# A weight ring of eight 2 MB places turned into four places of 4 MB

## The chip, the cores and the metric

The kernel runs on one core of a Trainium2 chip. The metric is the device time of one execution in microseconds (us). A core has five engines that run side by side: TensorE (PE in the rows; its weight loads are listed apart as PEld), VectorE (DVE), ScalarE (ACT), GpSimd (POOL) and SyncE (SP). Here SP mostly issues transfers. Sixteen DMA engines move the data; each transfer is spread over all of them, and a transfer adds 16 to its semaphore when it has landed.

## The reference

One decoder layer is computed for 256 prompt tokens and 8 sample tokens, 264 in all, with a model width of 1024, in float32. An attention and a recurrent branch are added to the input. Then each token goes through 4 of 32 experts and the results are added:

```
x += mix(x)
x += sum over the token's top 4 of 32 experts: gate * expert(rmsnorm(x))
expert(v) = act(v @ w_gate_up) @ w_down      # w_gate_up 1024 x 2048, w_down 1024 x 1024
```

The activation is a clamped SwiGLU of the gate and the up columns. One expert's weights are 8 MB (gate-up) and 4 MB (down), so 32 experts have 384 MB, each byte of which is read once. With 64 token slots to an expert, no expert overflows in these inputs.

## The kernel before

The first 172 us compute the two branches, the router and the choice of tokens. After that TensorE works through 16 pairs of experts. A pair gathers 64 tokens for each of two experts into one tile of 128 and transposes it (`x_transposes`). For each of the two experts it then does `gate_up` (line 1554: 32 matmuls of 64 tokens by 512 columns, contraction in 8 blocks of 128, and 4 bias matmuls), `act_transposes` (line 1575: 4 transposes of 128 by 128 that turn the activated tile around) and `down` (line 1582: 16 matmuls). Beside the matmuls VectorE and ScalarE compute the activation and copy results out of PSUM. Between the two halves of a pair TensorE adds the results of the pair before to the tokens (`place_half`, `place_quarters`, lines 1596 to 1605) and gathers the tokens of the next pair (line 1493). In the trace one float32 matmul is two MATMUL instructions, and one transpose is one.

The weights come through a ring of eight places of 2 MB: six in a buffer of their own, one in the tail of `regA`, one in the head of `regX`. An expert is six pieces: four of gate-up, which hold two consecutive rows per partition, and two of down, with four rows per partition. SP issues piece n+8 when TensorE has counted piece n as used (`m_used`); TensorE counts a gate-up piece after 8 matmuls and a down piece after 8. TensorE waits for a piece by the semaphore of its place (`landed`, line 1545).

Before the experts start the ring is filled as far as memory is free. Pieces 0 to 3 are issued at the start. Pieces 4 and 5 lie where the attention branch had its scratch (`scr`) and are issued when that branch is done. Pieces 6 and 7 lie in `regX` and `regA` and are issued when the router is done. From then on the loop at line 343 takes over:

```
sp.wait_ge(m_used, u * (4 * PIECES) + (n + 1))
load_piece(n % SLOTS, u * 4 + x, j)
```

Of the kernel before, what the change touches and what calls it, by code (L numbers as in the profile page):

```python
# [25 lines left out]
P = 128  # L26
D = 1024
KT = D // P
NP_ = 256
NS = 8  # L30
T = NP_ + NS
# [4 lines left out]
NC = 4  # L36
# [3 lines left out]
FF = 1024  # L40
D_IN = 1792
CAP = 64
N_OVER = 16
ITEMS = E + N_OVER
PIECES = 6
GU = 4
SLOTS = 8
PIECE = 4 * FF
POS0 = 4096
EPS = 1e-6  # L50
SCALE = HD ** -0.5
# [23 lines left out]
def hybrid_layer(nc, a, o):  # L75

    ctx = ExitStack()
    with ctx:
        def sb(name, shape, dt=F32):
            return ctx.enter_context(nc.sbuf_tensor(name, shape, dt))  # L80
# [1 line left out]
        def sem(name):  # L82
            return ctx.enter_context(nc.semaphore(name))

        ring = sb("ring", [P, 6, PIECE])
        regA = sb("regA", [P, KT * D_IN + 5 * T + NC * (3 + NP_)])
        con = sb("con", [P, NCONST])
        x_row = sb("x_row", [P, NT, D])
        xq = sb("xq", [P, D // 4])
        regX = sb("regX", [P, KT * T + 2 * NC * T])  # L90
        hT_t = regX[:, 0:KT * T]
        regC = regX[:, KT * T:]
        regD = regA[:, KT * D_IN:]
# [24 lines left out]
        ps = ctx.enter_context(nc.psum_tensor("ps", [P, 8, 512], F32))  # L118
# [4 lines left out]
        ident = cc("ident")  # L123
# [20 lines left out]
        up_sb = regA[:, 3072:3584]  # L144
        sig_sb = regA[:, 3584:4096]
        act_sb = regA[:, 4096:4608]
        actT = regA[:, 4608:5120].rearrange("p (j t) -> p j t", j=4)

        y_sb = [regA[:, 2048:2560], regA[:, 5120:5632]]

# [5 lines left out]
        xg = x_row[:, 2, :]  # L156
# [10 lines left out]
        idxg = chosen(694, 3)  # L167
        tail = KT * D_IN + 5 * T + NC * (3 + NP_)

        slot = [ring[:, s, :] for s in range(6)] + [regA[:, tail - PIECE:tail], regX[:, 0:PIECE]]  # L170

        def at(x, j):
            return divmod(PIECES * x + j, SLOTS)

        scr = ring[:, 4:6, :].rearrange("p s n -> p (s n)")
        diag_x = [scr[:, P * i:P * i + P] for i in range(NT)]
        v0 = scr[0:KT, 384:512]
        st10 = scr[0:10, 1400:1400 + T]
# [39 lines left out]
        s_slot = [sem(f"slot_landed{j}") for j in range(SLOTS)]  # L218
# [45 lines left out]
        def _(sp):  # L264
# [28 lines left out]

            def load_piece(s, e, j):
                if j < GU:
                    src = w_gu[bass.ds(e * D + j * 2 * P, 2 * P), :].rearrange("(p t) n -> p t n", t=2)
                    sp.dma_start(slot[s].rearrange("p (t n) -> p t n", t=2), src).then_inc(s_slot[s], 16)
                else:
                    src = w_dn[bass.ds(e * FF + (j - GU) * 4 * P, 4 * P), :].rearrange("(p t) n -> p t n", t=4)
                    sp.dma_start(slot[s].rearrange("p (t n) -> p t n", t=4), src).then_inc(s_slot[s], 16)  # L300

            def load_first(i):
                load_piece(i, i // PIECES, i % PIECES)

            for i in range(4):
                load_first(i)

            sp.wait_ge(S["proj"], 14)
# [13 lines left out]

            sp.wait_ge(S["pv"], 2)
            sp.wait_ge(S["ms_o"], 1)
            load_first(4)
            sp.wait_ge(S["s_pv"], 1)
            sp.wait_ge(s_cout, 32)
            load_first(5)

            sp.wait_ge(S["out_r"], 5)  # L330
            for odd in range(2):
# [2 lines left out]
            sp.dma_start(tokens, a["tokens"][:, :]).then_inc(s_tok, 16)  # L334
            sp.dma_start(bias_dn, a["b_down"][0]).then_inc(s_tok, 16)
            sp.wait_ge(S["logit"], NT)
            load_first(7)
            sp.wait_ge(S["xn"], 1)
            sp.wait_ge(S["xw"], 6)
            sp.wait_ge(S["st_tr"], 3)  # L340
            load_first(6)

            with sp.Fori(0, E // 4 - 1) as u:
                for n in range(4 * PIECES):
                    x, j = divmod(SLOTS + n, PIECES)
# [133 lines left out]
        def _(act):  # L479
# [204 lines left out]

            def copy_act(q):
                act.wait_ge(m_atr, q + 1)
                act.activation(actT[:, :, :], ps[:, 3, :].rearrange("p (j t) -> p j t", j=4),
                               ACT.Copy).then_inc(m_aT, 1)

            def bias_gu(odd, e):  # L690
# [32 lines left out]
            with act.If(n_over > 0):  # L723
                with act.Fori(0, n_over) as m:
                    for odd in range(2):
                        e = act.value_load(ovi[0:1, bass.ds(m * 2 + 1 + odd, 1)], min_val=0, max_val=E - 1)
# [463 lines left out]
        def _(pe):  # L1190
            def transpose(out, in_, k):
                return pe.transpose(out, in_, ident[0:k, 0:k])  # L1192
# [32 lines left out]
            for n in range(len(order) + 1):  # L1225
# [9 lines left out]
                kt = order[n - 1]  # L1235
# [4 lines left out]
                for m in range(6):  # L1240
                    mm = product(m, 2 + m, kt)
# [44 lines left out]
            for n, w in ((0, 128), (1, 256)):  # L1286
                for c in range(4):
                    for g in range(2):
                        h = 4 * g + c
                        out = ps[:, 2 + h // 2, 256 * (h % 2):256 * (h % 2) + 256] if n else ps[:, 6 + g, P * c:P * c + P]  # L1290
                        mm = pe.matmul(out, qk[64 * g:64 * g + 64, c, P * n:P * n + P],
                                       qk[64 * g:64 * g + 64, 4, 0:w], start=True, stop=True)
# [43 lines left out]
            for j, (n, kb, g) in enumerate(groups):  # L1336
# [43 lines left out]
            for b in range(NS):  # L1380
                r = slice(8 * b, 8 * b + 8)
# [145 lines left out]
            def x_transposes(g, half):  # L1527

                pe.wait_ge(m_xr, 2 * g + (half + 1))
                pe.sem_inc(m_passed, 1)  # L1530
                for j in range(4):
                    c = 512 * half + 2 * P * (j // 2) + j % 2
                    mm = transpose(ps[:, 7 - half, P * j:P * j + P], xg[:, c:c + 2 * P - 1:2], P)
                mm.then_inc(m_xtr, 1)

            def slot_sums():
# [8 lines left out]
            def landed(r, x, j, over):  # L1545

                again, s = at(x, j)
                if over:
                    pe.wait_ge(s_slot[s], r * (32 if s < 2 * PIECES - SLOTS else 16) + (E // 4 * 48 + 16 * again + 16))
                else:  # L1550
                    pe.wait_ge(s_slot[s], r * 48 + (16 * again + 16))
                return slot[s]

            def gate_up(p, r, x, over):

                odd = x % 2
                for kt in range(KT):
                    if kt % 2 == 0:
                        w = landed(r, x, kt // 2, over)
                    for n in range(2):  # L1560
                        for h in range(2):
                            c = 2048 * (kt % 2) + 1024 * h + 512 * n
                            mm = pe.matmul(ps[64 * h:64 * h + 64, 1 + n, :], xT[:, kt, 64 * odd:64 * odd + 64],  # L1563
                                           w[:, c:c + 512], start=(kt == 0), stop=False)
                    if kt % 2:
                        mm.then_inc(m_used, 1)
                pe.wait_ge(s_bgu[odd], p * 32 + 32)
                pe.sem_inc(m_passed, 1)
                for n in range(2):
                    for h in range(2):  # L1570
                        mm = pe.matmul(ps[64 * h:64 * h + 64, 1 + n, :], selb[32 * n:32 * n + 2, h, :],  # L1571
                                       b_gu[odd][32 * n:32 * n + 2, :], start=False, stop=True)
                mm.then_inc(m_gu, 1)

            def act_transposes(q):

                pe.wait_ge(m_act, q + 1)
                for j in range(4):
                    mm = transpose(ps[:, 3, P * j:P * j + P], act_sb[:, j:j + 4 * P - 3:4], P)
                mm.then_inc(m_atr, 1)  # L1580

            def down(p, r, x, over, ahead=False):

                pe.wait_ge(m_aT, p * 2 + (x % 2 + 1))
                for h in range(2):
                    w = landed(r, x, GU + h, over)
                    for j in range(4):
                        for n in range(2):
                            mm = pe.matmul(ps[64 * n:64 * n + 64, 4, :], actT[:, j, 64 * h:64 * h + 64],  # L1589
                                           w[:, 1024 * j + 512 * n:1024 * j + 512 * n + 512],  # L1590
                                           start=(h == 0 and j == 0), stop=(h == 1 and j == 3))
                    mm.then_inc(m_used, 1)
                    if ahead and h == 0:
                        x_transposes(p + 1, 1)

            def place_quarters(lhs, rhs):

# [156 lines left out]
```

## Time and profile before

| what | us |
|---|---|
| median of three runs | 1121.16 (1119.91 to 1129.12) |
| the profiled execution, its own time | 1119.43 |
| span of its trace | 1117.5 |
| TensorE busy in the span | 1062.6 |
| VectorE, ScalarE, GpSimd busy | 323.7, 152.3, 53.6 |
| DMA read from memory | 420.06 MB, 378 GB/s over the span |

Times inside the trace count from the start of the span. What lies around it is 1.9 us. Matmuls are pipelined, so that a TensorE that is shown as busy may still have room. Where TensorE waits for a piece, the row of the matmul tells so in brackets with the idle time before it.

### The profile page before, as it was taken

Reading aid. Unit: us, or ns where it says so; the run is one execution under the profiler, and the core shown is the slowest. Engines: PE = TensorE matmul, PEld = TensorE weight load, DVE = VectorE, ACT = ScalarE, POOL = GpSimd, SP = SyncE. Lnnn points to the kernel's source line nnn. Section 1 sums busy time; section 2 is a strip of 40 time slices with the busy share of each in tenths; the row PEclk is TensorE's granted clock in tenths of the full one; section 3 lists DMA queues with packets and bytes.
Section 4 is the critical chain, followed back from the end, with each engine's and each line's share of the span. In section 5 each row is a group of like instructions: output and inputs, shape, how many; then the busy total and the mean of one; then the engine's idle time right before and its main releaser. Section 6 shows DMA issues by size and latency. Waiting matters only on the chain.

```text
span 1117.5 us, 12869 instructions
## 1 busy us (share of the span) xinstructions
PE 1062.6 (95%) x4987; PEld 429.5 (38%) x4987; DVE 323.7 (29%) x653; ACT 152.3 (14%) x284; POOL 53.6 (5%) x85
## 2 busy tenths in 40 slices
PE   5999988999999999999999999999999999999996
PEld 4676453343333343433332333333333333233322
DVE  1482569113131313131313131313131312213132
ACT  1145331010101010101010101010101101010100
POOL 4063020000000000000000000000000000000000
PEclk9999888899999999999999999999999999999998
DMA  9906327699999999999999999999999999999991
GB/s 334 382 17 180 151 103 308 287 425 429 427 428 427 427 429 427 429 429 427 429 428 427 428 429 428 427 428 428 428 428 428 428 428 430 427 428 428 426 427 72
DMA packets 33020, 421.75 MB, mean 377 GB/s; under 512 B 4466, under 2 KB 4962, under 8 KB 8398
## 3 DMA queue, kind: packets, MB, share of 16 engines
q1 hardware_dynamic: 31486, 418.34, 89.2%
q0 software_dynamic: 1264, 2.75, 0.8%
q8 instruction: 21, 0.34, 0.1%
q10 hardware_dynamic: 240, 0.25, 0.1%
q14 instruction: 9, 0.07, 0.0%
HBM read 420.06 MB, written 2.33 MB: 378 GB/s over the span
## 4 chain that ended last, share of the span: by engine, by line
PE 67%; DMA 28%; DVE 3%; issue 1%; ACT 0%; SPq 0%; DVEq 0%; ACTq 0%
DMA ring<-in_w_gate_up_dram 26%; PE ps L1563 24%; PE ps L1589 15%; PE ps L1493 8%; PE ps L1216 3%; PE ps L1192 3%; PE ps L1605 3%; PE ps L1390 3%; PE ps L1571 2%; PE ps L1219 2%; DMA regA<-in_w_out_dram 1%; PE ps L1540 1%; PE ps L1202 1%; DMA x_row<-in_x_prompt_dram 1%; PE ps L1408 0%
## 5 line engine op out<-in xcount | busy, mean ns | idle before, releaser
L1563 PE MATMUL ps<-ring,regA 128*64 128x512 f32 x1536 | 341.5, 596 | 22.4 <-DMA ring<-in_w_gate_up_dram 22.3
L1563 PEld LDWEIGHTS ps<-ring,regA 128*64 128x64 f32 x1536 | 108.6, 137 | 249.9 <-issue 203.8
L1589 PE MATMUL ps<-ring,regA 128*64 128x512 f32 x768 | 173.4, 601 | 0.1
L1142 DVE TENSOR_SCALAR regA<-ps 128x512 f32<-128x512 f32 x32 | 22.1, 691 | 422.2 <-PE ps L1571 422.2
L683 ACT ACTIVATE regA<-regA 128x512 f32<-128x512 f32 x32 | 20.2, 630 | 675.2 <-DVE regA L1142 675.2
L1156 DVE COPY regA<-ps 64x512 f32<-64x512 f32 x64 | 44.1, 688 | 205.2 <-PE ps L1589 204.2
L1589 PEld LDWEIGHTS ps<-ring,regA 128*64 128x64 f32 x768 | 53.1, 138 | 106.6 <-issue 98.7
L1493 PE MATMUL ps<-regA 128*128 128x512 f32 x192 | 88.5, 610 | 0.0
L1605 PE MATMUL ps<-regA 128*128 128x512 f32 (+1 forms) x136 | 69.2, 634 | 0.0
L1563 PE MATMUL ps<-regX,regA 128*64 128x512 f32 x256 | 58.0, 595 | 0.5 <-DMA regX<-in_w_gate_up_dram 0.2
L1563 PE MATMUL ps<-regA 128*64 128x512 f32 x256 | 57.6, 592 | 0.0
L1493 PEld LDWEIGHTS ps<-regA 128*128 128x128 f32 x192 | 35.8, 193 | 51.0 <-issue 51.0
L1136 DVE TENSOR_TENSOR x_row<-x_row,ps 128x512 f32<-128x512 f32 x68 | 42.4, 682 | 4.5 <-PE ps L1605 3.9
L1216 PE MATMUL ps<-regX,regA 128*128 128x264 f32 x160 | 39.2, 395 | 0.0
L1571 PE MATMUL ps<-regA,con 2*64 2x512 f32 x256 | 34.8, 613 | 0.0
L1605 PEld LDWEIGHTS ps<-regA 128*128 128x128 f32 (+1 forms) x136 | 24.3, 199 | 26.0 <-issue 26.0
L1390 PE MATMUL ps<-regA,regX 128*128 128x512 f32 x64 | 31.8, 649 | 1.4 <-DMA regA<-in_w_out_dram 1.4
L1216 PEld LDWEIGHTS ps<-regX,regA 128*128 128x128 f32 x160 | 29.8, 192 | 8.4 <-issue 3.9
L1563 PEld LDWEIGHTS ps<-regX,regA 128*64 128x64 f32 x256 | 17.6, 137 | 39.2 <-issue 31.4
L1563 PEld LDWEIGHTS ps<-regA 128*64 128x64 f32 x256 | 18.4, 137 | 36.6 <-issue 36.6
L1589 PE MATMUL ps<-regA 128*64 128x512 f32 x128 | 30.8, 625 | 0.7 <-issue 0.7
L1192 PEld LDWEIGHTS ps<-con,regA 128*128 128x128 f32 (+3 forms) x141 | 21.5, 195 | 20.6 <-DVE regA L1150 9.4
(280 smaller groups left out, 717.3 us busy)
## 6 DMA issues: line engine op xcount, KB each, us to landing
ring<-in_w_gate_up_dram SPq DMA_DIRECT2D x96, 2048.0 KB, 29.8
ring<-in_w_down_dram SPq DMA_DIRECT2D x48, 2048.0 KB, 34.3
regX<-in_w_gate_up_dram SPq DMA_DIRECT2D x16, 2048.0 KB, 29.9
regA<-in_w_gate_up_dram SPq DMA_DIRECT2D x16, 2048.0 KB, 29.2
regA<-in_w_down_dram SPq DMA_DIRECT2D x8, 2048.0 KB, 34.0
regX<-in_w_down_dram SPq DMA_DIRECT2D x8, 2048.0 KB, 35.4
regA<-in_w_in_dram SPq DMA_DIRECT2D x8, 896.0 KB, 12.2
regA<-in_w_out_dram SPq DMA_DIRECT2D x2, 1024.0 KB, 10.5
```

What stands on the lines that cost most here:

```text
L1136: dve.tensor_tensor(half, half, ps[:, PLACE[i][h], :], ALU.add).then_inc(m_add, 1)
L1142: dve.tensor_scalar(g_sb, gu[:, 0::2], LIMIT, None, ALU.min).then_inc(m_g, 1)
L1156: dve.tensor_copy(y_sb[n][64 * odd:64 * odd + 64, :], ps[64 * n:64 * n + 64, 4, :]).then_inc(m_ysb, 1)
L1192: return pe.transpose(out, in_, ident[0:k, 0:k])
L1216: return pe.matmul(ps[:, bank, 0:T], w_in[:, kt, P * n:P * n + P], hT[:, kt, :], start=(kt == 0), stop=(kt == KT - 1))
L1219: mm = pe.matmul(ps[64 * g:64 * g + 64, bank, 0:T], w_in[:, kt, 256 * g + 64 * n:256 * g + 64 * n + 64], hT[:, kt, :], start=(kt == 0), st ...
L1390: mm = pe.matmul(ps[:, bank, :], src[:, c, P * i:P * i + P], w_out[:, NC * half + c, 512 * n:512 * n + 512], start=(c == 0), stop=(c == NC ...
L1493: return pe.matmul(ps[:, 5 * half, :], oneh[:, i, :], xn_row[:, i, 512 * half:512 * half + 512], start=(i == 0), stop=(i == 1))
L1563: mm = pe.matmul(ps[64 * h:64 * h + 64, 1 + n, :], xT[:, kt, 64 * odd:64 * odd + 64], w[:, c:c + 512], start=(kt == 0), stop=False)
L1571: mm = pe.matmul(ps[64 * h:64 * h + 64, 1 + n, :], selb[32 * n:32 * n + 2, h, :], b_gu[odd][32 * n:32 * n + 2, :], start=False, stop=True)
L1589: mm = pe.matmul(ps[64 * n:64 * n + 64, 4, :], actT[:, j, 64 * h:64 * h + 64], w[:, 1024 * j + 512 * n:1024 * j + 512 * n + 512], start=(h ...
L1605: return pe.matmul(ps[:, PLACE[i][h], :], lhs[:, P * i:P * i + P], rhs[h], start=True, stop=True)
```

## The change

The ring has four places of 4 MB. Three are in a buffer of their own; the fourth joins the tail of `regA` to the head of `regX`, which are now one tensor. An expert is three pieces: two of gate-up with four rows per partition, and the whole down block with eight rows per partition. The same bytes are in the ring and the same bytes are moved, in 96 transfers instead of 192. A piece is counted as used after 16 matmuls instead of 8.

With eight rows per partition the down block needs the activated tile in another order. The 4 transposes become 16 ordinary matmuls with the identity on 64 by 64 quarters of the array: for each of eight column offsets one for each half of the partitions. A semaphore increment is added in front of them. The token transposes step by four columns instead of two.

```
-PIECES = 6
-GU = 4
-SLOTS = 8
-PIECE = 4 * FF
+PIECES = 3
+GU = 2
+SLOTS = 4
+PIECE = 8 * FF
...
-        slot = [ring[:, s, :] for s in range(6)] + [regA[:, tail - PIECE:tail], regX[:, 0:PIECE]]
+        slot = [ring[:, s, :] for s in range(3)] + [regAX[:, tail - PIECE // 2:tail + PIECE // 2]]
...
             def load_piece(s, e, j):
                 if j < GU:
-                    src = w_gu[bass.ds(e * D + j * 2 * P, 2 * P), :].rearrange("(p t) n -> p t n", t=2)
+                    src = w_gu[bass.ds(e * D + j * 4 * P, 4 * P), :].rearrange("(p t) n -> p t n", t=4)
...
-                    src = w_dn[bass.ds(e * FF + (j - GU) * 4 * P, 4 * P), :].rearrange("(p t) n -> p t n", t=4)
+                    src = w_dn[bass.ds(e * FF, FF), :].rearrange("(p t) n -> p t n", t=8)
...
-            for i in range(4):
+            for i in range(2):
                 load_first(i)
...
             sp.wait_ge(S["pv"], 2)
             sp.wait_ge(S["ms_o"], 1)
-            load_first(4)
             sp.wait_ge(S["s_pv"], 1)
             sp.wait_ge(s_cout, 32)
-            load_first(5)
+            load_first(2)
...
             sp.wait_ge(S["logit"], NT)
-            load_first(7)
             sp.wait_ge(S["xn"], 1)
             sp.wait_ge(S["xw"], 6)
             sp.wait_ge(S["st_tr"], 3)
-            load_first(6)
+            load_first(3)
...
                 for j in range(4):
-                    c = 512 * half + 2 * P * (j // 2) + j % 2
-                    mm = transpose(ps[:, 7 - half, P * j:P * j + P], xg[:, c:c + 2 * P - 1:2], P)
+                    c = 512 * half + j
+                    mm = transpose(ps[:, 7 - half, P * j:P * j + P], xg[:, c:c + 4 * P - 3:4], P)
...
                 for kt in range(KT):
-                    if kt % 2 == 0:
-                        w = landed(r, x, kt // 2, over)
+                    if kt % 4 == 0:
+                        w = landed(r, x, kt // 4, over)
...
-                    if kt % 2:
+                    if kt % 4 == 3:
                         mm.then_inc(m_used, 1)
...
             def act_transposes(q):
 
                 pe.wait_ge(m_act, q + 1)
-                for j in range(4):
-                    mm = transpose(ps[:, 3, P * j:P * j + P], act_sb[:, j:j + 4 * P - 3:4], P)
+                pe.sem_inc(m_passed, 1)
+                for t in range(8):
+                    for h in range(2):
+                        r = slice(64 * h, 64 * h + 64)
+                        mm = pe.matmul(ps[r, 3, 64 * t:64 * t + 64], act_sb[r, t:t + 8 * 64 - 7:8], ident[r, r], start=True, stop=True)
                 mm.then_inc(m_atr, 1)
 
             def down(p, r, x, over, ahead=False):
 
                 pe.wait_ge(m_aT, p * 2 + (x % 2 + 1))
-                for h in range(2):
-                    w = landed(r, x, GU + h, over)
-                    for j in range(4):
-                        for n in range(2):
...
-                    mm.then_inc(m_used, 1)
-                    if ahead and h == 0:
+                w = landed(r, x, GU, over)
+                for t in range(8):
+                    for n in range(2):
+                        mm = pe.matmul(ps[64 * n:64 * n + 64, 4, :], actT[:, t, :], w[:, 1024 * t + 512 * n:1024 * t + 512 * n + 512],
+                                       start=(t == 0), stop=(t == 7))
+                    if ahead and t == 3:
                         x_transposes(p + 1, 1)
+                mm.then_inc(m_used, 1)
```

## Rows read from the trace of the kernel before

**Rows 1.** The page: DMA's busy share in tenths, in 40 slices of the span.
```profile
DMA  9906327699999999999999999999999999999991
```

**Rows 2.** Busy time by stretch; last three columns: granted clock, DMA share, GB/s.
```profile
core 0: us, PE busy (x) PEld busy (x) DVE busy (x) ACT busy (x) POOL busy (x), PEclk, DMA share, GB/s
...
200.00:210.00 10.00, 10.00 (x38) 2.97 (x38) 1.78 (x3) 0.00 (x0) 0.00 (x0) 0.80 0.24 70
210.00:220.00 10.00, 10.00 (x48) 3.23 (x46) 1.63 (x4) 0.00 (x0) 0.00 (x0) 1.00 1.00 429
220.00:230.00 10.00, 10.00 (x42) 4.05 (x39) 2.67 (x4) 1.64 (x3) 0.00 (x0) 1.00 1.01 432
250.00:1050.00 800.00, 779.41 (x3564) 282.57 (x3562) 190.02 (x347) 81.46 (x125) 0.00 (x0) 1.00 1.01 428
...
1090.00:1100.00 10.00, 6.33 (x32) 2.08 (x29) 2.67 (x4) 1.23 (x2) 0.00 (x0) 0.91 0.17 72
```

**Rows 3.** The chain of waits by time: start, length, what (gate-up is L1563).
```profile
239.00 13.73 PE ps L1563 x64
...
519.03 13.73 PE ps L1563 x64
...
575.00 6.89 PE ps L1563 x32
582.05 32.56 DMA ring<-in_w_gate_up_dram
...
634.12 6.89 PE ps L1563 x32
...
1049.81 6.89 PE ps L1563 x32
```

**Rows 4.** SP's timeline, 100 to 216 us: issues of weight pieces, merged.
```profile
112.77 0.82 SPq L300 DMA_DIRECT2D ring<-in_w_down_dram  x2
...
160.36 0.37 SPq L297 DMA_DIRECT2D regA<-in_w_gate_up_dram  x1
177.80 3.73 SPq L297 DMA_DIRECT2D ring<-in_w_gate_up_dram  x2
184.62 3.80 SPq L300 DMA_DIRECT2D ring<-in_w_down_dram  x2
206.69 3.30 SPq L297 DMA_DIRECT2D ring<-in_w_gate_up_dram  x2
```

**Rows 5.** TensorE's timeline, 170 to 215 us: transposes and down of expert 0.
```profile
197.80 1.13 PE L1192 MATMUL ps<-con,regA 128*128 128x128 f32 x4
...
200.86 8.60 PE L1589 MATMUL ps<-ring,regA 128*64 128x512 f32 x32
```

**Rows 6.** TensorE's timeline at the end, 1049 to 1118 us, expert 31.
```profile
1084.50 3.65 PE L1563 MATMUL ps<-ring,regA 128*64 128x512 f32 x16 [1.25 <-DMA ring<-in_w_gate_up_dram]
1089.38 3.65 PE L1563 MATMUL ps<-ring,regA 128*64 128x512 f32 x16 [1.23 <-DMA ring<-in_w_gate_up_dram]
1092.97 1.09 PE L1571 MATMUL ps<-regA,con 2*64 2x512 f32 x8
1096.99 0.75 PE L1192 MATMUL ps<-con,regA 128*128 128x128 f32 x4 [2.93 <-DVE regA L1150]
1098.47 5.21 PE L1589 MATMUL ps<-regA 128*64 128x512 f32 x16 [0.73 <-issue]
```

**Rows 7.** The chain of waits, 250 to 330 us: four transposes each.
```profile
290.71 0.68 PE ps L1192 x4
...
313.04 0.47 PE ps L1192 x4
```

**Rows 8.** TensorE's groups by line and shape: count, busy us, mean ns of one.
```profile
L1493 PE MATMUL ps<-regA 128*128 128x512 f32 x192 | 88.5, 610 | 0.0
...
L1291 PE MATMUL ps<-regA 64*128 64x256 f32 x16 | 1.9, 376 | 0.0
...
L1291 PE MATMUL ps<-regA 64*128 64x128 f32 x16 | 1.2, 285 | 1.1 <-DVE regA L805 1.1
```

**Rows 9.** The page: the instruction queue's packets, MB and share.
```profile
q8 instruction: 21, 0.34, 0.1%
```

More of the change, by code:

```diff
@@ L83, in sem @@
             return ctx.enter_context(nc.semaphore(name))
-        ring = sb("ring", [P, 6, PIECE])
-        regA = sb("regA", [P, KT * D_IN + 5 * T + NC * (3 + NP_)])
+        ring = sb("ring", [P, 3, PIECE])
+        regAX = sb("regAX", [P, KT * D_IN + 5 * T + NC * (3 + NP_) + KT * T + 2 * NC * T])
+        regA = regAX[:, 0:KT * D_IN + 5 * T + NC * (3 + NP_)]
+        regX = regAX[:, KT * D_IN + 5 * T + NC * (3 + NP_):]
         con = sb("con", [P, NCONST])
@@ L89, in hybrid_layer @@
         xq = sb("xq", [P, D // 4])
-        regX = sb("regX", [P, KT * T + 2 * NC * T])
         hT_t = regX[:, 0:KT * T]
@@ L146, in hybrid_layer @@
         act_sb = regA[:, 4096:4608]
-        actT = regA[:, 4608:5120].rearrange("p (j t) -> p j t", j=4)
+        actT = regA[:, 4608:5120].rearrange("p (j t) -> p j t", j=8)
         y_sb = [regA[:, 2048:2560], regA[:, 5120:5632]]
@@ L168, in hybrid_layer @@
         tail = KT * D_IN + 5 * T + NC * (3 + NP_)
-        slot = [ring[:, s, :] for s in range(6)] + [regA[:, tail - PIECE:tail], regX[:, 0:PIECE]]
+        slot = [ring[:, s, :] for s in range(3)] + [regAX[:, tail - PIECE // 2:tail + PIECE // 2]]
         def at(x, j):
             return divmod(PIECES * x + j, SLOTS)
-        scr = ring[:, 4:6, :].rearrange("p s n -> p (s n)")
+        scr = ring[:, 2, :]
         diag_x = [scr[:, P * i:P * i + P] for i in range(NT)]
@@ L295, in load_piece @@
                 if j < GU:
-                    src = w_gu[bass.ds(e * D + j * 2 * P, 2 * P), :].rearrange("(p t) n -> p t n", t=2)
-                    sp.dma_start(slot[s].rearrange("p (t n) -> p t n", t=2), src).then_inc(s_slot[s], 16)
-                else:
-                    src = w_dn[bass.ds(e * FF + (j - GU) * 4 * P, 4 * P), :].rearrange("(p t) n -> p t n", t=4)
-                    sp.dma_start(slot[s].rearrange("p (t n) -> p t n", t=4), src).then_inc(s_slot[s], 16)
+                    src = w_gu[bass.ds(e * D + j * 4 * P, 4 * P), :].rearrange("(p t) n -> p t n", t=4)
+                    sp.dma_start(slot[s].rearrange("p (t n) -> p t n", t=4), src).then_inc(s_slot[s], 16)
+                else:
+                    src = w_dn[bass.ds(e * FF, FF), :].rearrange("(p t) n -> p t n", t=8)
+                    sp.dma_start(slot[s].rearrange("p (t n) -> p t n", t=8), src).then_inc(s_slot[s], 16)
             def load_first(i):
                 load_piece(i, i // PIECES, i % PIECES)
-            for i in range(4):
+            for i in range(2):
                 load_first(i)
@@ L686, in copy_act @@
                 act.wait_ge(m_atr, q + 1)
-                act.activation(actT[:, :, :], ps[:, 3, :].rearrange("p (j t) -> p j t", j=4),
+                act.activation(actT[:, :, :], ps[:, 3, :].rearrange("p (j t) -> p j t", j=8),
                                ACT.Copy).then_inc(m_aT, 1)
@@ L1557, in gate_up @@
                 for kt in range(KT):
-                    if kt % 2 == 0:
-                        w = landed(r, x, kt // 2, over)
+                    if kt % 4 == 0:
+                        w = landed(r, x, kt // 4, over)
                     for n in range(2):
                         for h in range(2):
-                            c = 2048 * (kt % 2) + 1024 * h + 512 * n
+                            c = 2048 * (kt % 4) + 1024 * h + 512 * n
                             mm = pe.matmul(ps[64 * h:64 * h + 64, 1 + n, :], xT[:, kt, 64 * odd:64 * odd + 64],
                                            w[:, c:c + 512], start=(kt == 0), stop=False)
-                    if kt % 2:
+                    if kt % 4 == 3:
                         mm.then_inc(m_used, 1)
@@ L1584, in down @@
                 pe.wait_ge(m_aT, p * 2 + (x % 2 + 1))
-                for h in range(2):
-                    w = landed(r, x, GU + h, over)
-                    for j in range(4):
-                        for n in range(2):
-                            mm = pe.matmul(ps[64 * n:64 * n + 64, 4, :], actT[:, j, 64 * h:64 * h + 64],
-                                           w[:, 1024 * j + 512 * n:1024 * j + 512 * n + 512],
-                                           start=(h == 0 and j == 0), stop=(h == 1 and j == 3))
-                    mm.then_inc(m_used, 1)
-                    if ahead and h == 0:
+                w = landed(r, x, GU, over)
[4 more added lines that the diff above has]
+                    if ahead and t == 3:
                         x_transposes(p + 1, 1)
+                mm.then_inc(m_used, 1)
             def place_quarters(lhs, rhs):
```

## The prediction

> **What bounds the kernel now.** I read the page's slices first: the DMA line stands at 9 from the eighth slice to the last but one [rows 1]. The table of stretches sharpens it: from 210 us on, the share is 1.00 to 1.01 at 428 to 432 GB/s, the 800 us from 250 to 1050 us run at 428, and only the last 10 us before the end fall to 72 [rows 2]. So for nearly 880 us all sixteen DMA engines always have work, and 2 MB take 4.90 us at that rate; two waiting matmuls at the end start 4.88 us apart [rows 6], which is the same thing seen from TensorE.
>
> The chain of waits says when TensorE joins. From 519.03 to 575.00 us a pair of experts took 55.97 us with no wait. The first wait for a piece comes at 582 us, and from there the pairs take DMA's pace: 59.12 us for the first, and 59.38 for each of the seven between 634.12 and 1049.81 [rows 3]. TensorE's reserve at the end is therefore 3.15 + 7 x 3.41 + the 1.25 and 1.23 us of the last expert [rows 6], 29.5 us. DMA bounds, but TensorE is only 5% behind it; this reserve decides what extra TensorE work is free.
>
> Two places lie outside the steady stretch. In front, between 200 and 210 us, DMA is 0.24 busy [rows 2]: all loads that places allowed are done, and the next waits for the first down half of expert 0, issued at 206.69 [rows 4]. At the end, TensorE needs the last gate-up piece at 1089.38 and then runs alone to the end [rows 6].
>
> **The change, part by part.** The sum goes against the profiled execution's 1119.43 us, which is 1.7 below the median of the three runs.
>
> *The early fills.* Pieces 4 and 5 were issued together at 112.77, pieces 6 and 7 just ahead of and at 160.36 [rows 4]. The joined ones go out at the later of each two: at most 0.5 us later, and TensorE needs none of them before 200 us. Zero, covered by the 47 us and the 40 us in between.
>
> *The ring's first turn.* Expert 0's four gate-up pieces each freed a place (177.80; 177.80 + 3.73 - 0.34 = 181.19; 184.62; 188.08). Now the first 4 MB go at 181.19 and the second at 188.08. Their 8 MB need 19.6 us and end near 203 instead of 200, still inside the DMA gap: free. Then it counts. Before, the first half of down freed a place at 206.69; now the whole block must be done, which was the second of the two issues in that row, 206.69 + 3.30 - 0.33 = 209.66 [rows 4]. The bytes moved up to that point are equal, 24 MB, so DMA's unbroken run starts 3.0 us later. The changed transposes lie in front of it on TensorE, where four transposes took 1.13 us instead of 0.47 and down 8.60 [rows 5]; at that pace I add 0.8. **+3.8 us.**
>
> *The next turn.* Expert 2's 12 MB then last from about 211.5 to 241. The next load needs the place of expert 1's down block, whose end was 239.00 [rows 3] and becomes 240.4 with two changed transposes, plus about 1 us until bytes flow: a gap of some 0.6 us. From there TensorE at 55.97 + 1.4 per pair draws ahead of DMA's 58.8, and no further gap opens. SP has only these loads queued behind its waits until the outputs. **+0.6 us.**
>
> *The transfers.* Ninety-six instead of 192, with twice the run per partition. No row shows a run of that length. The busy share already leaves nothing between packets, so what can be gained lies inside them. One end is 0; the other is the best 10 us in the table, 432 against 428, 0.9% of 880 us, 8 us. A loss isn't excluded by any row either; I bound it by the same 8 us. The mean of 800 us is nearest to no change; fewer completions per byte lean to gain. I take **-2 us.**
>
> *The transposes.* Four transposes take 0.47 us in the chain, and 0.68 where a semaphore increment stands before them [rows 7]. The sixteen matmuls are 32 instructions of 64 columns on two quarters of the array. The nearest row is the attention scores, on two halves of 64 partitions: 16 instructions of 128 columns kept TensorE 1.2 us, those of 256 columns 1.9 [rows 8]. At 64 columns I halve the first: 0.6 for 16, 1.2 for 32, less what its start adds, about 1.0; with 0.2 for the increment the addition is 0.7 per expert. The lower end is 0.3. The upper end is no overlap of the quarters: a 512-column instruction costs 88.5/192 = 0.46 us [rows 8], so 64 columns 0.058, 32 of them 1.85, an addition of 1.6; and if each weight load stood beside its matmul unhidden, 3.4. Over 31 experts 0.7 makes 22 us, which the reserve of 29.5 us, plus what DMA itself is later, hides. In the last expert nothing hides it. **+0.7 us.** The longer stride of the token transposes, the copy out of PSUM and the down matmuls keep their counts and shapes: zero.
>
> The writes of the two halves go to one PSUM bank. The Trainium skill's TensorEngine Tiling (Array Packing), section Restrictions and Gotchas, says that different row tiles cannot access the same bank at once. By that the two halves take turns; the scores' two halves wrote different banks, so no row here decides it. It is the first rival.
>
> *The instruction stream.* A round of the loop gains 112 matmuls and as many loads. The 21 packets of the page [rows 9] show that the loop isn't fetched every round; if it were, some 35 more such packets, 0.57 MB, cost DMA 1.3 us. I take 0.
>
> *The tail.* The last gate-up wait was for 2 MB, after which 16 instructions ran in 3.65 us; now it is for 4 MB, and 32 follow, 7.0 us. Where it lands relative to DMA's end is unchanged, since 4 MB of down follow in both. **+3.4 us.** From its start to down were 9.1 us [rows 6]; with 3.4 and 0.7 more it is 13.2, while the down block needs 9.8, so waiting for it whole costs nothing.
>
> Sum: 3.8 + 0.6 - 2 + 0.7 + 3.4 = 6.5 us; 1119.43 + 6.5 = 1125.9, say **1126 us.**
>
> **The rivals.**
>
> *TensorE becomes the bound (slower).* Without waits, TensorE would end at 1119.4 - 29.5 = 1089.9 plus 32 times the addition per expert. That passes 1126 from an addition of 1.1 us on. If the quarters run one after the other (1.5 to 1.6), the end is near 1139; with the loads unhidden as well (3.4), 1199. For it: the order of matmuls alternates quarters that share a bank, and a reserve of 5% is thin. Against it: in the trace two half-height tiles do overlap, 16 instructions of 128 columns in 1.2 us where one after the other at 0.115 each would be 1.84 [rows 8].
>
> *The longer runs move faster.* At 432 GB/s all through the 8 us come back: 1126 - 6 = 1120, and with the first-turn terms at their low ends 1117. For it: half the completions. Against it: a busy share that is full at 428.
>
> *A fixed cost per transfer is recovered (faster).* If every transfer held up its successors, 96 fewer would show. The trace speaks against it: piece follows piece at 4.88 us, the pace of the bytes [rows 6]. The Trainium skill's DMA: Bandwidth & Descriptors, section Anatomy of one DMA, gives about 2 us fixed beside the bytes; by that, as an estimate, 192 us would be saved and the time be near 930. What remains possible from rows is the difference between the 59.38 of a pair and 24 MB at 428, 58.8: 0.6 over 15 pairs, 9 us, which with the losses above gives 1117. Only an overlapping gain of both this and the rate would come below 1110.
>
> **How the numbers follow.** About 1% either way, 1109.9 to 1132.4 around 1121.16, is what a measurement can tell from no change. Forecast: 0.70, alone from 1121 to 1130. TensorE as the bound: 0.16, above 1132. Faster transfers: 0.09, and the fixed cost: 0.05, of which together 0.05 reach below 1109.9. So faster 0.05, same 0.79, slower 0.16. The range runs from 1116, where the faster transfers end, to 1138, which takes in quarters one after the other in their milder form.
>
> **What would show it.** Right: the gap of DMA before 210 us ends near 210.4 instead of 206.7; the stretch 250 to 1050 stays at 428 to 430 GB/s; pairs late in the run still take about 59 us with a wait for DMA in each; the last 32 gate-up instructions start after a wait and take 7 us; the new transposes take 1.0 to 1.3 us. Wrong: transposes of 1.8 us or more and pairs with no wait for DMA at the end (the first rival); a rate of 432 or more (the second); stretches below a full DMA share after 250 us, which would mean that four places are too few to keep it fed, a step I have at 0.6 us.

## The result: 2.3% slower, with TensorE as the bound

| | before | after |
|---|---|---|
| median, us (4 runs of each) | 1120.88 (1119.91 to 1129.12) | 1148.05 (1147.04 to 1150.27) |
| profiled execution, us | 1119.43 | 1147.51 |
| span, us | 1117.5 | 1145.6 |
| TensorE busy, us | 1062.6 | 1113.2 |

The ratio is 1.0232, with a 95% interval of 1.0188 to 1.0275. The prediction was 1126, with a range that ended at 1138.

The page of the changed kernel, first the engines' busy time, then DMA's tenths, then the shares of the chain that ended last (the work that finished last, followed back step by step to what released it):

```profile
PE 1113.2 (97%) x5883; PEld 478.5 (42%) x5883; DVE 324.8 (28%) x653; ACT 155.5 (14%) x284; POOL 54.1 (5%) x85
...
DMA  9907346699999999999999999999999999999971
...
PE 93%; DVE 4%; ACT 2%; issue 1%; DMA 0%; DVEq 0%; SPq 0%; ACTq 0%
```

DMA still looks full, as it did in [rows 1]. But the chain has nothing of it: TensorE waits for no piece of an expert.

The stretches of the changed kernel, with the columns of [rows 2]:

```profile
200.00:210.00 10.00, 10.00 (x36) 3.28 (x36) 1.28 (x2) 0.60 (x1) 0.00 (x0) 0.60 0.26 111
210.00:220.00 10.00, 10.00 (x50) 3.31 (x48) 2.12 (x4) 0.00 (x0) 0.00 (x0) 1.00 0.66 262
...
240.00:250.00 10.00, 10.00 (x50) 3.38 (x50) 2.02 (x4) 1.88 (x2) 0.00 (x0) 1.00 0.81 321
250.00:1050.00 800.00, 800.00 (x4224) 314.83 (x4222) 188.29 (x341) 80.85 (x119) 0.00 (x0) 1.00 1.00 423
```

TensorE is busy for all of the 800 us, where 779.41 stood before, and the rate is 423 GB/s instead of 428 [rows 2]. DMA's share reads 1.00 all the same, so a full DMA line alone doesn't say which side sets the pace; the rate and the waits do.

One pair of experts in the chain of waits of the changed kernel (start, length, what):

```profile
271.94 13.73 PE ps L1562 x64
...
286.69 5.35 PE ps L1492 x12
292.03 2.08 PE ps L1581 x32
294.11 0.68 PE ps L1191 x4
...
321.36 2.08 PE ps L1581 x32
323.44 1.05 PE ps L1605 x2
...
331.51 8.58 PE ps L1562 x39
```

The pair takes 331.51 - 271.94 = 59.57 us, where a pair without waits took 55.97 [rows 3]. L1581 are the 32 instructions of the small matmuls: 2.08 us, where the four transposes took 0.47 [rows 7]. The addition is 3.60 / 2 = 1.8 us per expert. Put into the formula of the prediction's first rival it gives 1089.9 + 32 x 1.8 = 1147.5 us, which is the time of the profiled execution.

Groups by shape in the changed kernel, weight loads and matmuls (count, busy us, mean ns of one, idle before):

```profile
L1562 PEld LDWEIGHTS ps<-ring,regAX 128*64 128x64 f32 x1536 | 110.6, 137 | 220.1 <-issue 220.0
...
L1581 PE MATMUL ps<-con,regAX 64*64 64x64 f32 x1024 | 68.8, 286 | 3.0 <-DVE regAX L1149 3.0
L1581 PEld LDWEIGHTS ps<-con,regAX 64*64 64x64 f32 x1024 | 64.3, 213 | 28.1 <-issue 28.1
```

A weight load of 64 columns takes 213 ns in L1581, and 137 in the gate-up line. The two also differ in their rows, 64 against 128; what stands out is that the columns of L1581 lie eight apart in the tile. Whether that is the cause, the experiments have to tell.

### The profile page after: what moved, and what is told of

Read it like the earlier page. It is cut to its first block, busy times and chain, and to the rows that moved or that the text cites. A ratio compares the mean times of both kernels' runs of the same rounds, so it can differ in the third digit from the quotient of the medians.

```text
span 1145.6 us, 14346 instructions
## 1 busy us (share of the span) xinstructions
PE 1113.2 (97%) x5883; PEld 478.5 (42%) x5883; DVE 324.8 (28%) x653; ACT 155.5 (14%) x284; POOL 54.1 (5%) x85
## 4 chain that ended last, share of the span: by engine, by line
PE 93%; DVE 4%; ACT 2%; issue 1%; DMA 0%; DVEq 0%; SPq 0%; ACTq 0%
PE ps L1562 37%; PE ps L1590 20%; PE ps L1492 7%; PE ps L1605 6%; PE ps L1581 6%; PE ps L1215 3%; PE ps L1570 3%; PE ps L1191 3%; PE ps L1218 2%; PE ps L1389 1%; PE ps L1599 1%; PE ps L1539 1%; PE ps L1201 1%; DMA x_row<-in_x_prompt_dram 0%; PE ps L1444 0%
## 5 line engine op out<-in xcount | busy, mean ns | idle before, releaser
L1562 PE MATMUL ps<-ring,regAX 128*64 128x512 f32 x1536 | 336.8, 595 | 0.0
L1562 PEld LDWEIGHTS ps<-ring,regAX 128*64 128x64 f32 x1536 | 110.6, 137 | 220.1 <-issue 220.0
L1590 PE MATMUL ps<-ring,regAX 128*64 128x512 f32 x768 | 174.5, 604 | 0.0
L1562 PE MATMUL ps<-regAX 128*64 128x512 f32 x512 | 112.6, 592 | 0.0
L1155 DVE COPY regAX<-ps 64x512 f32<-64x512 f32 x64 | 44.1, 689 | 222.5 <-PE ps L1590 221.5
L1590 PEld LDWEIGHTS ps<-ring,regAX 128*64 128x64 f32 x768 | 52.9, 138 | 107.4 <-issue 99.4
L1492 PE MATMUL ps<-regAX 128*128 128x512 f32 x192 | 88.4, 609 | 0.0
L1581 PEld LDWEIGHTS ps<-con,regAX 64*64 64x64 f32 x1024 | 64.3, 213 | 28.1 <-issue 28.1
L1581 PE MATMUL ps<-con,regAX 64*64 64x64 f32 x1024 | 68.8, 286 | 3.0 <-DVE regAX L1149 3.0
L1605 PE MATMUL ps<-regAX 128*128 128x512 f32 (+1 forms) x136 | 70.8, 646 | 0.0
L1590 PE MATMUL ps<-regAX 128*64 128x512 f32 x256 | 59.6, 610 | 0.7 <-issue 0.7
L1492 PEld LDWEIGHTS ps<-regAX 128*128 128x128 f32 x192 | 35.8, 193 | 50.8 <-issue 50.8
L1215 PE MATMUL ps<-regAX 128*128 128x264 f32 x160 | 39.5, 398 | 0.0
L1605 PEld LDWEIGHTS ps<-regAX 128*128 128x128 f32 (+1 forms) x136 | 24.1, 196 | 26.8 <-issue 25.6
L1389 PE MATMUL ps<-regAX 128*128 128x512 f32 x64 | 31.9, 652 | 1.9 <-DMA regAX<-in_w_out_dram 1.0
L1215 PEld LDWEIGHTS ps<-regAX 128*128 128x128 f32 x160 | 29.9, 193 | 8.5 <-issue 3.9
```

The source lines that it names most:

```text
L1155: dve.tensor_copy(y_sb[n][64 * odd:64 * odd + 64, :], ps[64 * n:64 * n + 64, 4, :]).then_inc(m_ysb, 1)
L1215: return pe.matmul(ps[:, bank, 0:T], w_in[:, kt, P * n:P * n + P], hT[:, kt, :], start=(kt == 0), stop=(kt == KT - 1))
L1389: mm = pe.matmul(ps[:, bank, :], src[:, c, P * i:P * i + P], w_out[:, NC * half + c, 512 * n:512 * n + 512], start=(c == 0), stop=(c == NC ...
L1492: return pe.matmul(ps[:, 5 * half, :], oneh[:, i, :], xn_row[:, i, 512 * half:512 * half + 512], start=(i == 0), stop=(i == 1))
L1581: mm = pe.matmul(ps[r, 3, 64 * t:64 * t + 64], act_sb[r, t:t + 8 * 64 - 7:8], ident[r, r], start=True, stop=True)
L1590: mm = pe.matmul(ps[64 * n:64 * n + 64, 4, :], actT[:, t, :], w[:, 1024 * t + 512 * n:1024 * t + 512 * n + 512], start=(t == 0), stop=(t = ...
```

## The experiments

The theory after the first comparison was that the loads of columns eight apart are what the transposes cost. Its rivals were that the larger ring costs part of the 27 us, that the two halves take turns at their common PSUM bank, and that small matmuls are dear in themselves. The ratios below are to the kernel before.

**The ring alone.** The places of 4 MB stay; the old four transposes come back. For that the down block is loaded with two runs of four rows per partition:

```
-src = w_dn[bass.ds(e * FF, FF), :].rearrange("(p t) n -> p t n", t=8)
+src = w_dn[bass.ds(e * FF, FF), :].rearrange("(h p t) n -> p h (t n)", h=2, t=4)
```

> The four places of 4 MB stay; the down block comes in one transfer but as two runs of four rows per partition, so that the four old transposes and the old order of the activated tile serve again. Theory 1, TensorE is bound by the sixteen small matmuls: a pair is back at 56.0 us where it doesn't wait, waits for DMA return late in the run, and the time is 1119.4 + 3.0 (first turn) + 3.4 (tail), less up to 5 us for the faster longer runs of gate-up: 1121 to 1126. Theory 2, four places are too few to keep DMA fed: 1140 or more, with DMA shares below 1.00 after 250 us and TensorE waiting for pieces.

Measured: 1124.99 us over 10 runs, ratio 1.0021 (0.9992 to 1.005); the profiled execution took 1124.32, with a span of 1122.4. Its stretch of 800 us, and the end of TensorE's timeline:

```profile
250.00:1050.00 800.00, 778.13 (x3548) 282.84 (x3544) 189.92 (x346) 80.84 (x124) 0.00 (x0) 0.99 1.00 430
```

```profile
1081.96 7.04 PE L1562 MATMUL ps<-ring,regAX 128*64 128x512 f32 x32
1089.82 7.09 PE L1562 MATMUL ps<-ring,regAX 128*64 128x512 f32 x32 [0.82 <-DMA ring<-in_w_gate_up_dram]
...
1100.86 1.13 PE L1191 MATMUL ps<-con,regAX 128*128 128x128 f32 x4 [2.94 <-DVE regAX L1149]
1102.72 9.31 PE L1587 MATMUL ps<-regAX 128*64 128x512 f32 x32 [0.73 <-issue]
```

DMA is the bound again, with a wait in front of the last 32 gate-up instructions. The terms that the prediction gave the ring can be read here one by one; that is done below.

**The transposes alone.** Eight places of 2 MB as before, but the down rows are laid out by eight and the small matmuls are in:

```
-src = w_dn[bass.ds(e * FF + (j - GU) * 4 * P, 4 * P), :].rearrange("(p t) n -> p t n", t=4)
+src = w_dn[bass.ds(e * FF, FF), :].rearrange("(p t) n -> p t n", t=8)[:, 4 * (j - GU):4 * (j - GU) + 4, :]
```

> The ring of eight places of 2 MB as before; only the down block's rows are laid out eight to a partition (two pieces of four of the eight), and the sixteen small matmuls take the place of the four transposes. Theory 1: TensorE never waits for a weight piece after 250 us, a pair takes 59.5 us, and the time is 1089.9 + 32 x 1.8 = 1147, between 1143 and 1151. Theory 2: within 4 us of the kernel before, 1117 to 1126.

Measured: 1148.64 us over 4 runs, ratio 1.0222 (1.0166 to 1.0278), against 1.0232 for the whole change. The stretch of 800 us in this kernel:

```profile
250.00:1050.00 800.00, 800.00 (x4224) 314.81 (x4222) 188.40 (x341) 80.88 (x119) 0.00 (x0) 1.00 1.00 423
```

TensorE is busy for the whole stretch and the rate is 423, as in the changed kernel. The transposes carry the whole loss. What the ring costs by itself lies in the part of DMA's time that TensorE now covers.

**Neighbouring columns.** The same 32 instructions, but each load takes 64 neighbouring columns:

```
-act_sb[r, t:t + 8 * 64 - 7:8]
+act_sb[r, 64 * t:64 * t + 64]
```

> The changed kernel, but the small matmuls load 64 neighbouring columns instead of every eighth, so that the activated tile arrives in a wrong order; the work is the same otherwise. If the stride of the load makes the 2.08 us: 0.9 to 1.1 us for the 32 instructions, a pair near 57.5 us, DMA waits return, 1119 to 1127. If load and matmul of one quarter simply follow each other (53 + 48 ns): 1.6 to 1.7 us, a pair of 58.8, 1132 to 1138. If neither: 2.08 us and 1147.

Measured: 1124.73 us over 8 runs, ratio 1.0027 (0.9989 to 1.0064). The groups of L1581:

```profile
L1581 PE MATMUL ps<-con,regAX 64*64 64x64 f32 x1024 | 38.4, 227 | 3.0 <-DVE regAX L1149 3.0
L1581 PEld LDWEIGHTS ps<-con,regAX 64*64 64x64 f32 x1024 | 33.9, 140 | 28.1 <-issue 28.1
```

In the chain the 32 instructions are:

```profile
577.83 1.08 PE ps L1581 x32
```

The loads take 140 ns instead of 213, the 32 instructions 1.08 us instead of 2.08, and late in the run TensorE waits for pieces again. Small matmuls are not dear in themselves.

**The halves in turn.** The order of the two loops is exchanged, so that eight matmuls of one half of the partitions are followed by eight of the other. Bank, loads and count stay:

```
-for t in range(8):
-    for h in range(2):
+for h in range(2):
+    for t in range(8):
```

> The changed kernel, with the loops over the eight offsets and the two halves swapped: all of one half, then all of the other. If the halves ran side by side in the changed kernel in spite of their common PSUM bank: about 32 x 0.12 = 3.8 us instead of 2.08, a pair near 63, 1195 to 1210. If they already took turns at the bank: 2.08 us again and 1147.

Measured: 1228.89 us over 2 runs, ratio 1.0922 (1.0849 to 1.0995). Matmuls of L1581, one expert's in the chain, and the stretch of 800 us:

```profile
L1581 PE MATMUL ps<-con,regAX 64*64 64x64 f32 x1024 | 117.2, 288 | 3.0 <-DVE regAX L1149 3.0
```

```profile
623.54 3.58 PE ps L1581 x32
```

```profile
250.00:1050.00 800.00, 800.00 (x3886) 333.99 (x3884) 172.43 (x312) 74.72 (x110) 0.00 (x0) 0.96 0.92 390
```

In turn they take 3.58 us per expert in the chain, against 2.08: in the change the work of the halves does overlap, though they write one bank. The run with neighbouring columns says so of the matmuls too: its 1.08 us is less than the 1.85 that the prediction worked out for quarters one after the other. The profiled execution took 81.8 us more than that of the changed kernel (1229.27 against 1147.51), and 32 x 1.5 accounts for only 48. The rest fits the granted clock (the share of its full clock that TensorE was given), which was 0.96 over the stretch: 0.04 of 800 us is 32. Other instructions of a pair took longer in places. That second part was not foreseen.

**Columns four and two apart.** The changed kernel with a step of four and, in a second run, of two in place of eight, one execution each:

```
-act_sb[r, t:t + 8 * 64 - 7:8]
+act_sb[r, 256 * (t // 4) + t % 4:256 * (t // 4) + t % 4 + 4 * 64 - 3:4]
```

```
-act_sb[r, t:t + 8 * 64 - 7:8]
+act_sb[r, 128 * (t // 2) + t % 2:128 * (t // 2) + t % 2 + 2 * 64 - 1:2]
```

> The changed kernel, but the small matmuls load every fourth column instead of every eighth (64 columns each as before; the activated tile arrives in a wrong order). If a load slows in proportion to its stride, between 1.08 us for the 32 instructions (neighbouring columns) and 2.08 (every eighth), about 1.5 us. If only strides beyond four cost, as the old transposes suggest, whose loads of 128 columns stepped by four and came 0.12 us apart: 1.1 to 1.2 us. If any stride costs the same: 2.08 us.

> The changed kernel with one thing different: each quarter loads 64 columns that lie two apart, where the change has them eight apart (the columns come in another order, so this measures the load's time alone). Any step costs the same: the 32 small matmuls take 2.05 to 2.1 us per expert, as with steps of eight and of four, TensorE waits for no piece, and the time is 1147 to 1149. The cost grows with the step up to four: about 1.4 to 1.6 us per expert, TensorE's end at 1089.9 + 32 x 1.2 to 1.3, and the time 1127 to 1133 with few waits for pieces left. Only a step of four or more costs: 1.08 us and about 1125, as with neighbouring columns.

Measured with a step of four: 1148.52 us, 2.06 us per expert. The groups of L1581:

```profile
L1581 PEld LDWEIGHTS ps<-con,regAX 64*64 64x64 f32 x1024 | 63.9, 211 | 28.1 <-issue 28.1
L1581 PE MATMUL ps<-con,regAX 64*64 64x64 f32 x1024 | 68.3, 285 | 3.0 <-DVE regAX L1149 3.0
```

With a step of two: 1128.01 us, beside one run of the kernel before at 1126.57 on the same chip; 1.11 us per expert. The same groups:

```profile
L1581 PEld LDWEIGHTS ps<-con,regAX 64*64 64x64 f32 x1024 | 34.8, 140 | 28.1 <-issue 28.1
L1581 PE MATMUL ps<-con,regAX 64*64 64x64 f32 x1024 | 39.2, 229 | 3.0 <-DVE regAX L1149 3.0
```

The expectation that any step costs the same held from eight to four and fell at two. Of float32 columns, neighbours and a step of two load in 140 ns, steps of four and of eight in 211 to 213. A step of three, or another type, wasn't tried. The Trainium skill's Advanced Engine Details and Errata, section Memory Cachelines, says that the on-chip memory is read in lines of 16 bytes, and that full speed needs at least two hits in a line. Four float32 are a line, so a step of two has two hits in each, and steps of four and eight have one: the four durations agree.

The ordinary transposes do not fit so simply. They too load the tile that they turn around. These are their weight loads by the tile that is read, in the kernel before and, last, in the changed kernel:

```profile
L1192 PEld LDWEIGHTS ps<-con,ring 128*128 128x128 f32 x32 | 3.6, 141 | 0.6 <-issue 0.4
L1192 PEld LDWEIGHTS ps<-con,regA 128*128 128x128 f32 x129 | 20.6, 204 | 19.6 <-DVE regA L1150 9.4 <-issue 8.6
L1192 PEld LDWEIGHTS ps<-con,x_row 128*128 128x128 f32 x144 | 19.8, 202 | 17.4 <-issue 13.2 <-DVE x_row L956 4.2
L1191 PEld LDWEIGHTS ps<-con,x_row 128*128 128x128 f32 x144 | 19.6, 202 | 18.4 <-issue 13.2 <-DVE x_row L955 4.2
```

Neighbouring columns took 141 ns, the activated tile with its step of four 204, and the tokens 202, both with a step of two before the change and with a step of four after it (16 of their 144 loads have neighbours). So here the border lies below a step of two, and the rule on lines alone doesn't account for it. Nor does the longer load show in the time: four token transposes take 0.68 us in the chain with either step.

**The order made by VectorE.** The multiply that ends the activation writes the tile in the order of the loads, so that they read neighbours and the result stays the same:

```
-dve.tensor_tensor(act_sb, up_sb, sig_sb, ALU.mult).then_inc(m_act, 1)
+dve.tensor_tensor(act_sb.rearrange("r (t p) -> r t p", t=8), up_sb.rearrange("r (p t) -> r t p", t=8),
+                  sig_sb.rearrange("r (p t) -> r t p", t=8), ALU.mult).then_inc(m_act, 1)
```

> The changed kernel with a right result and neighbouring columns: VectorE's last multiply of the activation writes the tile in the order in which the small matmuls load it, reading its two inputs with a step of eight. Theory 1 (the stride of the load is the cost): 1.08 us for the 32 instructions, a pair of 57.6 us, DMA bounds again late in the run, 1121 to 1128, and not slower than the kernel before by 1%. If the step of eight makes VectorE's 0.69 us much longer, the last expert's path gets longer by that once, and the other experts hide it: still under 1130.

Measured: 1126.34 us over 10 runs, ratio 1.0032 (1.0015 to 1.0049). The multiply in this kernel:

```profile
L1149 DVE TENSOR_TENSOR regAX<-regAX 128x512 f32<-128x512 f32 x32 | 34.7, 1085 | 1.1
```

The multiply takes 1085 ns instead of the 692 of the changed kernel; the small matmuls are at 1.08 us. This is the whole change with the dear loads taken out and a right result: the ratio falls from 1.0232 to 1.0032, so most of the loss is given back. VectorE's 0.4 us is hidden behind TensorE's other work but for the last expert, where TensorE waits 3.41 us for the activation instead of 3.02.

**The tail.** The ring alone, with the last gate-up piece of expert 31 as two transfers of 2 MB with a semaphore each, so that 16 instructions instead of 32 follow the last wait:

```
+if i == E * PIECES - 2:
+    load_half(i % SLOTS, i // PIECES, 1, 0, s_slot[i % SLOTS])
+    load_half(i % SLOTS, i // PIECES, 1, 1, s_half)
+    continue
...
+if last and kt == 6:
+    pe.wait_ge(s_half, 16)
```

> The ring alone with the old transposes (first experiment), and the last gate-up piece of the last expert comes as two transfers of 2 MB with a semaphore each. If waiting for the whole last piece is worth the 3.4 us of the prediction: 3 to 4 us less than the first experiment, 1119 to 1122. If the last wait is hidden anyway: no difference from the first experiment, 1124 to 1125.

Measured: 1123.85 us over 12 runs, ratio 1.0021 (1.0002 to 1.004); the profiled execution took 1121.42, 2.9 less than that of the ring alone. TensorE's timeline at the end:

```profile
1080.99 13.90 PE L1573 MATMUL ps<-ring,regAX 128*64 128x512 f32 x64
...
1100.40 8.68 PE L1598 MATMUL ps<-regAX 128*64 128x512 f32 x32 [0.81 <-DMA regAX<-in_w_down_dram]
```

The last wait for gate-up is gone. Between the profiled executions the tail gives back 2.9 of the predicted 3.4 us; the ratios to the kernel before are alike for the two, 1.0021 each, so the runs do not resolve it.

**The first turn too.** Besides, the first piece that goes into the place of expert 0's down block is issued as two halves, the first when half of that block is used:

```
+if n == 2:
+    sp.wait_ge(m_first, 1)
+    load_half(n, x, j, 0, s_slot[n])
+    sp.wait_ge(m_used, n + 1)
+    load_half(n, x, j, 1, s_h2)
+    continue
```

> As the run with the split tail, and the first piece that needs the place of expert 0's down block also comes as two transfers of 2 MB, the first of them issued when half of that block is used. If the prediction's 3.0 us for the first turn hold: another 2.5 to 3.5 us less, 1116 to 1119, which would be 0.2 to 0.5% faster than the kernel before. If DMA's start there doesn't set the end: the same as with the split tail alone.

Measured: 1123.62 us over 12 runs, ratio 1.0008 (0.9991 to 1.0025); the profiled execution took 1120.80. SP issues the half at 207.24 instead of the 211.51 of the run with the split tail, but the end comes only 0.6 us earlier, not the 2.5 to 3.5 expected. The stretches and, below them, one wait of TensorE near the end show where the rest went:

```profile
200.00:210.00 10.00, 10.00 (x33) 3.05 (x34) 1.28 (x2) 0.60 (x1) 0.00 (x0) 0.74 0.53 198
210.00:220.00 10.00, 10.00 (x50) 3.32 (x48) 2.12 (x4) 0.00 (x0) 0.00 (x0) 1.00 1.02 418
...
230.00:240.00 10.00, 10.00 (x52) 4.68 (x52) 0.16 (x1) 3.46 (x5) 0.00 (x0) 1.00 0.88 373
240.00:250.00 10.00, 10.00 (x50) 3.42 (x48) 2.02 (x4) 0.00 (x0) 0.00 (x0) 1.00 0.91 367
...
1030.00:1034.00 4.00, 4.00 (x14) 1.31 (x14) 0.00 (x0) 0.00 (x0) 0.00 (x0) 0.65 1.05 451
```

```profile
1029.85 8.78 PE L1587 MATMUL ps<-ring,regAX 128*64 128x512 f32 x32 [2.63 <-DMA ring<-in_w_gate_up_dram]
```

DMA starts 4.3 us earlier and then runs dry once more: between 230 and 250 us it lacks (1 - 0.88 + 1 - 0.91) x 10 = 2.1 us, where the run with the split tail alone has shares of 1.00 and 1.02. The issue that ends this gap comes only 0.8 us sooner, at 240.23 instead of 241.04. What is left reaches TensorE: the kernel without this edit resumes at 1031.81, after a wait of 1.21 us, this one at 1029.85. But here the wait was 2.63 us, the granted clock of the next 4 us is 0.65, and the 32 instructions take 8.78 us, where the other's take 7.09. That spends 1.7 of the 2.0 us.

No version of the four places is faster than the kernel before; the ring alone and the last one can't be told from it.

## Why the prediction was wrong, by its steps

**The transposes: the step that failed, by its size.** The term was 0.7 us per expert: 1.0 for the 32 instructions and 0.2 for the increment, less the 0.47 of the old transposes. Measured are 1.8 for the term and 2.08 for the 32 instructions. The row that I took, the attention scores [rows 8], gave the right price for loads of neighbouring columns: 1.08 us in the third experiment. It said nothing of a step of eight, and I gave the step no term, neither an end of the range nor a rival. The trace of the kernel before had a warning: the transposes' loads with a step took 202 to 204 ns, those without 141. The Trainium skill's rule on lines, cited above, is another. The reserve of 29.5 us, against which the term was set, held: it carries an addition of 0.9 per expert, and 1.8 is twice that. So the step that rested on the term fell too, that the reserve hides the 31 experts' additions: 32 x 1.8 is 57.6 us, 28.1 more than the reserve, and the profiled execution was 28.1 us longer.

**The 0.2 us for the increment** stood for something else. The small matmuls of the changed kernel start with no visible loss; what takes longer is the instruction behind them. L1605 takes 1.05 us, and the first four token transposes 0.68. In the chain of the kernel before, where the 128-column transposes stood ahead of it, the same L1605 was shorter:

```profile
313.51 0.86 PE ps L1605 x2
```

The 0.68 in [rows 7] likewise follows down matmuls of 64 columns. Where eight transposes stand in a row behind a 128-column gather, the second four with an increment in front, nothing is lost:

```profile
285.52 0.95 PE ps L1192 x8
```

So the 0.2 us goes with the passage from 64 columns to 128 and not with the increment, as far as these rows tell; no run took it apart.

**Rival one** had the outcome, the formula and the sign, at a chance of 0.16. Its mechanism fell, and that 1.8 lies between its prices of 1.6 and 3.4 is luck. The Trainium skill's TensorEngine Tiling (Array Packing), section Restrictions and Gotchas, was the ground for halves that take turns at a bank. The traces do not agree here: in turn they take 3.58 us, as the kernel has them 2.08, and 1.08 with neighbouring columns.

**The ring's terms**, read in the ring alone against the profiled execution before, 1124.32 against 1119.43, which is 4.9 us. These are two single executions; executions of the kernel before lie between 1119.4 and 1129.3 us, so the parts hold for these two traces only:

- First turn: predicted 3.8, of which 3.0 for the whole block and 0.8 for the transposes, which are not in this run. SP issues at 211.68 instead of 206.69 [rows 4], 5.0 later. But TensorE had begun expert 0 at 174.04 instead of 172.22, in a part that the ring's change leaves as it was; with the old ring and the small matmuls it began at 173.07. Counted from there the issue comes after 37.6 instead of 34.5 us: 3.2 of the 5.0 belong to the first turn, as predicted, and 1.8 to the part before it.
- Next turn: predicted 0.6. DMA's shares from 220 to 250 us are 0.97, 0.98 and 1.01, so that at most half a microsecond is missing. In the changed kernel the share of 0.81 from 240 to 250 us is a gap of 1.9, which TensorE, then the bound, doesn't notice.
- Transfers: predicted -2, ends 0 and -8. The last gate-up piece lands 0.44 us later than before (1089.82 against 1089.38 [rows 6]), though DMA began 5.0 later; so 4.6 us came back. The rate of 430 against 428 GB/s over 880 us is 4.1. The sign was right, the size was half. Whether the longer runs do it or the smaller number of transfers, no run separates.
- Tail: predicted 3.4. From the start of the last gate-up instructions to the end of the span are 1122.4 - 1089.82 = 32.6 us, before 1117.5 - 1089.38 = 28.1: 4.5 more. 3.4 are the 16 instructions. The rest goes with a lower granted clock behind them, 0.72 from 1100 to 1112 us against 0.86 from 1096 to 1108 before: the transposes take 1.13 instead of 0.75 us, and the down matmuls 9.31 instead of 8.65, from 1098.47 [rows 6] to the end of the row below.
- Together 5.0 - 4.6 + 4.5 = 4.9. The prediction's sum without the transposes' 0.7 and 0.8 is 3.0 + 0.6 - 2 + 3.4 = 5.0. That the two agree is luck: the transfers gave back 2.6 more than predicted, the tail cost 1.1 more, and 1.8 had come before the ring's first turn.

The last down matmuls of the kernel before, for the tail:

```profile
1103.50 3.62 PE L1589 MATMUL ps<-regX,regA 128*64 128x512 f32 x16
```

In the changed kernel itself these terms cost nothing that the runs show, because DMA no longer sets the end: without the ring the time was 1148.64 us, with it 1148.05. **The early fills** were free as predicted. **The instruction stream** was too: 24 packets instead of 21 [rows 9]; the 35 packets with which the prediction prices the other case come from no row. **Rival two** came about half way, with a rate of 430 to 431 GB/s where DMA was the bound, not 432. **Rival three** was not seen: a fixed cost for each transfer, if there is one, stays hidden under the queue. The Trainium skill's DMA: Bandwidth & Descriptors, section Anatomy of one DMA, gives the 2 us that the prediction cites for transfers issued by GpSimd; SP issues these.

**One reading** was off without touching the sum. The prediction has the first wait for a piece at 582 us. That time in [rows 3] is the start of a transfer at whose end TensorE waited. The first matmuls with such a wait are later:

```profile
609.76 3.65 PE L1563 MATMUL ps<-ring,regA 128*64 128x512 f32 x16 [1.24 <-DMA ring<-in_w_gate_up_dram]
614.65 3.65 PE L1563 MATMUL ps<-ring,regA 128*64 128x512 f32 x16 [1.24 <-DMA ring<-in_w_gate_up_dram]
```

## What to carry to other kernels

Where a layout is changed for longer DMA runs, look at who reads the tile in the new order. Price the stride of each operand as a term of its own: a row with the same shape and neighbouring columns bounds it from below only. And set the addition per turn against the reserve of the engine that is second: here the reserve was 5%, or 0.9 us per expert, and an addition of 1.8 made that engine the bound.

## What the runs showed of the hardware

- A weight load of 64 float32 columns on a quarter of the array takes 140 ns with neighbours or a step of two, 211 to 213 with a step of four or eight. The ordinary transposes of 128 columns load in 141 ns with neighbours and in 202 to 204 with a step of two or four, but their time in the chain is the same with a step of two and of four, 0.68 us for four.
- Two quarters that lie on the diagonal run side by side even into one PSUM bank: 2.08 us against 3.58 in turn, and 1.08 with neighbouring columns.
- VectorE's multiply of 128 by 512 takes 1085 ns instead of 692 when its two operands are read with a step of eight.
- Two waits of 1.25 and 1.23 us [rows 6] became one of up to 2.65 us. Behind some of these the granted clock of the next 4 us was 0.65, a mixture of the two levels of 2.4 and 1.2 GHz, and 32 instructions took 8.78 us instead of 7.09. The engine had been idle for 2.63 us before that. Behind another wait of 2.63 us they took 7.09, so the length of the wait by itself does not decide it. Both are in the ring alone:

```profile
617.51 7.09 PE L1562 MATMUL ps<-ring,regAX 128*64 128x512 f32 x32 [2.63 <-DMA ring<-in_w_gate_up_dram]
676.59 8.78 PE L1562 MATMUL ps<-ring,regAX 128*64 128x512 f32 x32 [2.65 <-DMA ring<-in_w_gate_up_dram]
```
